# A two-layer decoder step on one core: expert order, router form, page numbers, sample attention and copy queues changed together

## The reference: what is computed

```
grp = argmax(softmax(h @ w_group + b_group));  e_in = (h @ w_expert + b_expert)[group grp]
top_w, top_i = top_k(softmax(e_in), 2);  gates = g_w * top_w / sum(top_w)
h += sum_e gates[e] * ((silu(h @ w_gate[e]) * (h @ w_up[e])) @ w_down[e])
h += (p @ W_in) * sigmoid(rmsnorm(h) @ W_gate)
```

## Time and profile before

| | |
|---|---|
| median of 3 runs (lowest, highest) | 940.86 us (938.93, 948.01) |
| profiled execution: time, span, mean granted clock of PE | 949.18 us, 947.2 us, 0.924 |
| PE busy | 783.3 us (83%) |
| DVE, ACT, POOL busy | 319.4, 206.6, 56.0 us |
| DMA | 269.32 MB, 284 GB/s over the span |
| chain that ended last | PE 53%, DMA 23%, issue 13% |

### The profile page before, as it was taken

How to read it: one execution, slowest core, us unless ns; L and a number is a source line. 1 busy time by engine, 2 the same in 40 slices (tenths; PEclk the granted TensorE clock), 3 DMA queues, 4 the chain that set the end, 5 groups by cost and what they waited for, 6 DMA issues and landing times.

```text
span 947.2 us, 16693 instructions
## 1 busy us (share of the span) xinstructions
PE 783.3 (83%) x6434; PEld 566.7 (60%) x6434; DVE 319.4 (34%) x948; ACT 206.6 (22%) x490; POOL 56.0 (6%) x95
## 2 busy tenths in 40 slices
PE   5999789998777796989997685798997687778894
PEld 4876468765544464667774362588765355445683
DVE  2332134433221331255265271226233132213435
ACT  2100132512111111132135251015311111111222
POOL 5100000000000000000033232000000000000000
PEclk9999889999988988999999796799999898899997
DMA  9853716599999999974319074468699999999501
GB/s 376 300 174 79 249 51 256 191 420 406 415 417 416 415 418 417 418 292 145 122 60 358 22 236 140 171 229 321 270 399 419 415 418 415 418 416 415 225 1 46
DMA packets 59613, 269.32 MB, mean 284 GB/s; under 512 B 7312, under 2 KB 12704, under 8 KB 38416
## 3 DMA queue, kind: packets, MB, share of 16 engines
q1 hardware_dynamic: 53232, 259.37, 69.0%
q10 hardware_dynamic: 3712, 5.35, 1.9%
q0 software_dynamic: 2592, 3.54, 1.3%
HBM read 261.05 MB, written 2.52 MB: 278 GB/s over the span
## 4 chain that ended last, share of the span: by engine, by line
PE 53%; DMA 23%; issue 13%; POOLq 4%; DVE 3%; ACT 1%; ACTq 1%; POOL 1%; SPq 0%; DVEq 0%
DMA ring<-in_moe_w_up 22%; PE bank L483 16%; PE bank L623 15%; PE bank L602 5%; POOLq L1857 3%; PE bank L649 3%; PE bank L664 3%; PE bank L507 3%; PE bank L892 2%; DMA ring<-in_stream 1%; PE bank L558 1%; PE bank L544 1%; PE bank L467 1%; POOLq L1859 1%; POOLq L1856 1%
## 5 line engine op out<-in xcount | busy, mean ns | idle before, releaser
L623 PE MATMUL bank<-ring,arena 128*32 128x256 f32 x2048 | 148.1, 436 | 63.5 <-DMA ring<-in_moe_w_up 61.2
L623 PEld LDWEIGHTS bank<-ring,arena 128*32 128x32 f32 x2048 | 86.8, 125 | 130.3 <-issue 108.1
L483 PE MATMUL bank<-xn_sq,ring 128*128 128x264 f32 x480 | 110.3, 392 | 10.9 <-DMA ring<-in_stream 10.9
L483 PE MATMUL bank<-arena,ring 128*128 128x264 f32 (+1 forms) x456 | 109.6, 401 | 6.5 <-ACT arena L1597 4.0
L483 PEld LDWEIGHTS bank<-xn_sq,ring 128*128 128x128 f32 x480 | 92.5, 193 | 27.8 <-issue 11.7
L1229 DVE TENSOR_TENSOR arena<-arena,bank 128x128 f32<-128x128 f32 x34 | 9.8, 288 | 288.4 <-ACT arena L1638 288.4
L483 PEld LDWEIGHTS bank<-arena,ring 128*128 128x128 f32 x456 | 90.3, 199 | 23.7 <-issue 7.0
L602 PEld LDWEIGHTS bank<-arena 128*128 128x128 f32 x864 | 97.9, 192 | 9.4 <-issue 9.4
L602 PE MATMUL bank<-arena 128*128 128x128 f32 (+1 forms) x864 | 101.1, 277 | 2.0 <-DVE arena L1199 2.0
L649 PE MATMUL bank<-ring,arena 128*32 128x512 f32 x512 | 65.4, 598 | 16.6 <-ACT arena L1645 16.5
L664 PE MATMUL bank<-arena 128*128 128x264 f32 (+1 forms) x288 | 70.5, 399 | 4.7 <-ACT arena L1654 4.7
(11 more groups left out here) (243 smaller groups left out, 790.2 us busy)
## 6 DMA issues: line engine op xcount, KB each, us to landing
ring<-in_moe_w_gate SPq DMA_DIRECT2D x60, 1024.0 KB, 14.0
ring<-in_moe_w_up SPq DMA_DIRECT2D x60, 1024.0 KB, 10.7
ring<-in_moe_w_down SPq DMA_DIRECT2D x60, 1024.0 KB, 12.9
ring<-in_stream SPq DMA_DIRECT2D x35, 1024.0 KB, 12.5
ring<-in_cache_ckv SPq DMA_DIRECT2D x32, 256.0 KB, 7.6
arena<-in_moe_w_down SPq DMA_DIRECT2D x4, 1024.0 KB, 13.3
arena<-in_cache_ckv SPq DMA_DIRECT2D x16, 256.0 KB, 4.1
xn_sq<-in_cache_ckv SPq DMA_DIRECT2D x16, 256.0 KB, 5.5
```

The costliest lines, as they stand in the source:

```text
L483: t = mm(ps[:, 0:cols], lhs(k), rhs(k), start=(k == 0), stop=(k == n - 1))
L623: t = mm(bank[2 + r][p0:p0 + U, 0:F].rearrange("p (c f) -> p c f", c=2), x, w[i][:, :, k * F + c * P:k * F + (c + 1) * P], start=(k == 0), ...
```

## The change

Five parts, made at once.

- **Expert order.** The two-unit experts become pairs 8 and 9 (group 4) and are loaded there; pair 16, alone in the last group, becomes experts 28 and 29. Its `gate_up` and `turn_hid` move behind the last but one `combine`. The number of pieces, pairs and groups is the same.
- **Router.** The logits hold the 36 weight columns still and move 264 tokens past them, 8 matmuls, six of them between the `pw2` or `wo` chunks; a copy and 3 small transposes turn them. The squares are summed by 9 one-column matmuls straight into columns; the root is taken on 3 columns instead of 264. Five `pin` chunks of layer 0 move ahead of `pw2`; of the rest two stand ahead of the count in layer 0, three in layer 1. `route` gains one small DVE step.
- **Page numbers.** SP reads group 0's after its fill of `G_UQ` and group 1's right after group 0's loads; POOL reads 32 numbers at a time ahead of the loops, which become straight code.
- **Second sample group** after i = 12, 14, 16, 18, the first after i = 2, 4, 6, 8.
- **Last pair's copies** go to SP (6), ACT (5) and POOL (5); SP loads no expert piece until all 16 have landed. The last two `taps` chunks have two `means` between them.

```diff
+DOUBLE = 8
+WINDOW = [0, 1, 2, 3, -1, 4, 5, 6, 7]
-SAMPLE_AT = [3, 5, 7, 9]
+SAMPLE_AT = [[2, 4, 6, 8], [12, 14, 16, 18]]
-for _e in range(NSTAT + 1, E, 2):
+for _e in [*range(NSTAT + 1, 2 * DOUBLE, 2), NSING, *range(2 * DOUBLE, NSING, 2)]:
     MOE_PIECES += both(_e)
+PIN_EARLY = 5
+PIN_FIRST = [(5, 6), (0, 1, 2)]
+PIN_LAST = [(7,), (3, 4, 5, 6, 7)]
...
+        def copies(eng, p):
+            if p < PAIRS - 1:
+                return {"sp": every[:8], "act": every[8:], "pool": []}[eng]
+            return {"sp": every[:6], "act": every[6:11], "pool": every[11:]}[eng]
...
+            def logits(l, norm, k):
+                if k == 0:
+                    open_bank(pe, ("router", l))
+                    pe.wait_ge(s_wr, 32)
+                pe.wait_ge(s_xn, KD * norm + k + 1)
+                t = mm(bank[taken["router", l][0]][0:G + E, 0:T], wr[:, l, k, :], xnT[:, k, :], start=(k == 0),
+                       stop=(k == KD - 1))
...
+            def router_tail(l, norm):
+                logits(l, norm, KD - 2)
+                token_sums(l, 0)
+                token_sums(l, 1)
+                logits(l, norm, KD - 1)
+                token_sums(l, 2)
+                ps = open_bank(pe, ("lg", l))
+                freed(pe, ("router", l))
+                for i, (t0, n) in enumerate(TILES):
+                    t = mm(ps[0:n, LG * i:LG * i + G + E], lgT[:, t0:t0 + n], ident[0:G + E, 0:G + E], start=True,
+                           stop=True)
...
-            taps(PAIRS - 1)
-            means(range(KD // 2, KD)).then_inc(is_full("lnm"), 1)
+            taps(PAIRS - 1, (0,))
+            means((KD - 4, KD - 3))
+            taps(PAIRS - 1, (1,))
+            means((KD - 2, KD - 1)).then_inc(is_full("lnm"), 1)
+            pin(0, (0,))
             sum_squares("lnv", sq, KD, SQ["ln"])
+            pin(0, range(1, PIN_EARLY))
...
+                if 0 < m < KD - 1:
+                    logits(0, 1, m - 1)
...
-                    if j == NGR - 2:
-                        gate_up(NPR - 1)
                     down(b)
-                turn_hid(NPR - 1)
                 combine(NGR - 2)
...
+                gate_up(NPR - 1)
+                turn_hid(NPR - 1)
                 down(NPR - 1)
                 combine(NGR - 1)
...
+            def column_root(l):
+                key = ("router", l)
+                ps = arrive(act, key)
+                s.copy(lgT, ps[0:G + E, 0:T]).then_inc(is_free(key), 1)
+                freed(act, ("sums", l))
+                s.activation(rcol[:], rcol[:], ACT.Sqrt).then_inc(s_rs, 1)
...
+            shift_blocks(pool, "pool", PAIRS - 1)
...
-                    with pool.Fori(0, PAGES) as n:
-                        pg = pool.value_load(pages[0:1, bass.ds(n + (SB * B + i) * PAGES, 1)], min_val=0,
-                                             max_val=NPOOL - 1)
+                    for n in range(PAGES):
...
             moe(0)
+            pool.wait_ge(s_pg, 16)
+            numbers = page_numbers(0)
...
-            load_kpe(0)
+            load_kpe(numbers)
+            numbers = page_numbers(1)
...
+            copied(sp, PAIRS - 1)
             expert_stream(0)
-            for g in range(G_PG0, G_PIN1 - 1):
+            for g in range(G_PG0, G_UQ + 1):
                 fill(g)
             sp.wait_ge(s_pg, 16)
+            numbers = [page_numbers(i) for i in range(SB)]
+            for g in range(G_UQ + 1, G_PIN1 - 1):
+                fill(g)
...
             for B in range(TS // SB):
-                numbers = [page_numbers(SB * B + i) for i in range(SB)]
                 for i in range(SB):
                     load_cache(SB * B + i, numbers[i])
+                if B == 0:
+                    numbers = [page_numbers(SB + i) for i in range(SB)]
```

226 lines of the change are left out of this document (122 added, 104 removed).

## The result

| | median (lowest, highest), runs | ratio of the two |
|---|---|---|
| before | 940.25 us (938.93, 948.01), 4 | |
| changed | 921.44 us (920.66, 925.37), 4 | 0.9759, 95% interval 0.9718 to 0.9800 |

The ratio is changed over before, both measured side by side on one chip. The change makes the kernel faster, by 19 us and not by 56; 921.4 lies outside the range of 872 to 899. On two other chips the ratio was 0.9712 (0.9644 to 0.9779) and 0.9701 (0.9643 to 0.9759): there the changed kernel had medians of 918.96 and 919.92 us, and the kernel before 943.5 to 948.8 in five sets of 7 to 11 runs.

A forecast was written before the change was run, and what follows sets the result against it. Weight-stream restart and tail bound the experts, PE and its wait chains the rest. Gains of 24.5 us (layer 0), 17.9 (attention) and 13.4 (layer 1) sum to 55.8, taking the median 940.86 to 885.1 us; range 872 to 899.

The forecast's parts named there:

- Expert order, layer 0: End of layer 0's experts: the new order starts the embedding 11 us sooner after the stream's end, bounds -6 and -13.
- the embedding starts at T+10 to T+11: Experts' tail: after `gate_up`(16) ends at T+1.5, chain, `down`, copy and `combine` lead to the embedding, against T+21.1 in layer 0.
- T: End of the experts' weight stream, at 2.53 us a piece; 394.2 in layer 0 before; unmoved while a slot is free.
- The median: Whole kernel: the gain of 55.8 us, summed on the profiled 949.18 us, is taken unchanged from the median 940.86.
- Second group between heads: Attention: second sample group placed among the heads brings "so" to 588.3 instead of 606.22, -17.9 us, bounds -12 and -24.
- I take 18: Attention, from the end of the second scores to "so": heads and group chain overlap to 18 us, between 14 and 26.
- rival 1: Attention: the second group's wait at i = 12 blocks heads 13 to 15; attention gives 10, total 893 us; chance 0.14.
- Layer 0's router: Start to layer 0's first gather: copies 6.5, early `pin` 3.0, logits -2.7 and router 6.7 make it 13.5 us earlier.
- Logits: In `pw2` and `wo`: six matmuls of 264 columns at 0.44 us on PE's full path cost +2.7 us per layer.
- Early `pin`: Ahead of `pw2`, layer 0: chunks fill PE's 4.02 us wait and keep the clock, -3.0 us, bounds 0 and -3.5.
- Layer 1: Layer 1's router and experts: router 6.05, logits -2.7 and expert order 10 sum to a gain of 13.4 us.
- POOL can issue closer: Page loops: 0.65 us a page instead of 1.5; rival 4, that POOL cannot, gave 995 us, chance 0.02.

The follow-up runs named there:

- no_branch: Changed kernel without PE's branch to the general path in both layers, PE's part of that path left out: 914.91 us, ratio 0.963.
- old_expert_order: Changed kernel with the expert order of before, two-unit experts last and `gate_up`(16) behind `turn_hid`(15): 927.72 us.
- skipped_arm_longer: Changed kernel with 26 (layer 0) and 13 (layer 1) more matmuls in PE's general path, which is skipped: 926.14 us.
- skipped_arm_shorter: Changed kernel with 16 matmuls fewer per layer in PE's general path, which is never taken: 914.79 us, ratio 0.9711.
- group1_at_end: Changed kernel with the second sample group's four stages behind the last head, as in the kernel before: 908.93 us.
- logits_in_threes: Changed kernel with the six early logit matmuls in two lots of three, behind chunks 3 and 6, in both layers: 918.28 us.
- pin_all_behind: Changed kernel without early `pin` chunks: in layer 0 three ahead of the token count and five behind it: 921.73 us.
- attention_a_pin_once: Changed kernel with group 1's stages last, logits in threes, group 0 after i = 2, 4, 5, 7, layer 0's `pin` chunks 6 and 7 computed twice: 911.67 us.

## Why the prediction was wrong

The forecast was 36.3 us too low. The steps, by size:

- **Expert order, layer 0: -11 forecast, +0.8 came (11.8).** The stream ended where it was forecast to, and no slot was late. The step that failed is "the embedding starts at T+10 to T+11": it started at T+21.4. 2.3 us are T itself: by the landings the tail of the kernel before was 18.2 to 18.4 us and not 21, so there was less to gain, and `gate_up`(15) started at T-17.7 by the prediction's T, not at T-20. 2.1 are its own low clock behind an idle wait of 5.34 us (5.78 against 3.66, granted clock 0.62). The rest, some 7.5, is the wait behind the branch (2.7) and the clock behind it; beside no_branch it is 8.1 (39.1 against 31.0 from `gate_up`(15) to the embedding). The prediction had no term for the branch, since in the kernel before nothing waited there. That was the place of the code and not the order of the work (old_expert_order). Shown by no_branch, skipped_arm_longer and skipped_arm_shorter.
- **The median (9.1).** I took the gain from 940.86 "as it is". The sum was made from the rows of an execution of 949.18 us; against that it said 893.4, so 27.3 of the 36.3 lie in the sum. In the set of the result the two medians differ by 18.8 us, but the two profiles by 28.5, and the medians on two other chips by 29.1 and 27.6. Where the executions of some 940 us are shorter no profile shows. The other four points add to 29.8; the weights that came 2.1 us sooner go off that.
- **Second group between heads: -17.9 forecast, -11.4 came (6.5).** Each arrival was right within 1.3 us: first scores at 505.5 (forecast 504.2, which is 513.2 less the 9.0 us of layer 0), second at 554.6 (553.7), scores 7.8 (7.6). The step that failed is "I take 18" between the ends of 14 and 26: 22.8. That is most of the way to rival 1, and it hid a worse mistake, shown by group1_at_end: the move itself costs 10 us. The page numbers and group 0's place alone bring 22.6 (193.2 to 170.6 from the embedding to `wo`).
- **Layer 0's router: -13.5 forecast, -7.7 came (5.8).** Copies -6.3 for -6.5. Gather -6.4 to the last chunk for -6.7. Logits +4.6 for +2.7: 0.44 was the row's price for a full stationary, and 0.31 more is paid at each switch, shown by logits_in_threes. Early `pin`: 1.4 at `pw2` for 3.0 by pin_all_behind (2.1 against the kernel before), and the gather behind two idle waits took 2.6 more, which I had not counted.
- **Layer 1: -13.4 forecast, -7.7 came (5.7).** Logits again, +1.9. `wo`: the first 32 records took 10.01 us at a granted clock of 0.73 where at full clock they take 7.1; of these 2.9 us the kernel before lost 1.9 too, so +1.0. Router: its part brought 4.5 for 6.05, +1.6, since five `pin` chunks behind the count kept PE busy until 0.5 us before the gather. The tail: -6.8 for -10, by the same reading of T and the same slow `gate_up`(15). And 1.9 came at the end that I hadn't named; that stretch took 36.4 to 38.7 us in the variants, also where nothing in it had changed, so it may be none of the change's.

Right were the directions, the copies, the page price (0.57 for 0.65), the stream without a hole, and that POOL can issue closer.

One rule bore on the largest miss, and the prediction did not use it. The wait in layer 0 ends 5.9 us after the end of `combine`(7), the last work ahead of the branch, with a 16 KB packet of the instruction queue inside it. The Trainium skill, "Runtime: NRT & Kernel Launch", "Instruction fetch mechanics", says that "Branching breaks sequential prefetch": a jump to code outside what is held forces a fetch, and code comes in blocks of 16 KB. The traces agree in the size of the packet, in the edge that moves with the code, one record for each added, and in the packet's end 1.3 to 1.9 us ahead of each go-on; the page has no price for this, and here it was 0 to 6.1 us.

Open: why the low clock behind 6.13 us of standing still (skipped_arm_longer) lasted one `gate_up` (5.41, then `down` 1.92), and behind 2.71 us in the changed kernel through `down` and `combine`; why a packet had come before the branch in some runs and not in others; and whether emptier DMA queues shorten the wait, as the three cases suggest. None was tried.

## What to carry to other kernels

Look at each branch that is skipped: time what follows it in the trace, and treat "free so far" as a property of the code's length. Take the end of a stream of loads from the landings that the engine waits for, and not from the DMA rate: here they were 2.5 us and more apart. Put long skipped parts where the engine waits anyway, or keep them short. Before queuing a chain of waits between other work, ask what stands behind its wait: a wait of 12 us with 12 us of ready work behind it is a loss, however well the rest overlaps. A filled wait keeps the clock only until the next unfilled one.

## What the hardware showed that I had not expected

- PE stood still 0 to 6.1 us behind a skipped branch, by where the code lay; 52 records of never executed code more made 2.6 us into 6.1, 32 fewer made it none. Each wait ended 1.3 to 1.9 us after a 16 KB packet of instructions.
- Switching between a stationary of 128 columns and one of 36 cost 0.31 us for a matmul of 0.445 (4.32 a chunk with one, 3.56 without; three in a lot 1.45).
- `gate_up`(15) behind an idle wait of 5.2 to 5.7 us took 5.0 to 6.4 us, and 3.66 with that wait filled up to 1.45 us. Waits of 3.5 to 3.9 us ahead of it gave both: 4.9 to 6.4 us four times, and 3.66 once (attention_a_pin_once, layer 1, behind 3.90).
- The packet of instructions after a branch began 3.5 us or more behind it at 348 GB/s and above, and 1.1 to 1.6 us behind it at 0 to 21 GB/s.
